# First norm tile by tile between modulation units, and the sum of squares inside the last unit

## The chip, the cores and the metric

The kernel runs on one core of one Trainium2 chip. The metric is the device time in microseconds of one execution; the time before is the median of three executions.

## The reference

Two blocks follow one another. The first is a two-layer transformer over a sequence of 256 tokens (x) and a context of 256 tokens (ctx), width 1024. The second is a two-layer attention network over x alone; the change does not touch it. What matters of the first block:

```
mod = silu(c) @ w_mod[i] + b_mod[i]          # 6 x 1024 per layer; mod_c the same from c_ctx
sh1, sc1, g1, sh2, sc2, g2 = split(mod, 6)
h  = rms_norm(x,  g_pre_mix) * (1 + sc1) + sh1        # "norm mix"
u  = h @ w_in                                          # kv, q, bc, xs0, ... in columns
y  = concat(attention, short conv, state space) @ w_out
x  = x + g1 * rms_norm(y, g_post_mix)                  # "post mix"
h  = rms_norm(x, g_pre_ffn) * (1 + sc2) + sh2          # "norm ffn"
x  = x + g2 * rms_norm(square(relu(h @ w_ff1)) @ w_ff2, g_post_ffn)   # "post ffn"
```

The context goes through the same steps with its own modulation in layer 0; in layer 1 only its mixer inputs are needed.

## The kernel before

Activations stand transposed: eight tiles k = 0 to 7 of 128 features by 512 tokens (context and x; 256 tokens where x alone is left, in layer 1). All large products are done in three matmuls, high part by high part, low by high, high by low (L976 to L978): every operand is split into a rounded half (hi) and the rest (lo). For weights ACT makes whi (L1498) and VectorE (DVE) makes wlo by a subtraction (L2048), half a unit at a time, into four buffers. For a normalised tile ACT makes HH (hi) and H32 (the full value), and DVE subtracts to HL (L2070).

The work is a list of steps, written out by hand, and each of the engines walks through the same list in order and does its own part of a step. A *unit* is 256 columns of a weight matrix: one load of 1 MB (SP's queue, three raw buffers, so a unit's load waits until the unit three places earlier has released its buffer), the splits, and matmuls over the eight k. A *modulation unit* (kind mod) is 256 columns of w_mod; its parts are steps of their own where the unit is alone: `mod_mm` (TensorE's matmuls from the raw weights, L1012), `mod_row` (ACT copies the row, L1683), `mod_pick` (TensorE turns the row into columns, L997), `mod_col` (DVE copies them, L2259). `fuse_pair j` (DVE, two small instructions) makes the scale and shift of tiles 2j and 2j+1 from units j and 4 + j.

In the first norm (layer 0, mix), units 0, 4, 1 and 5 have been made before, so tiles 0 to 3 can be modulated. `split_to` and `split_hi` split weight halves up to a number. A `norm` step lets DVE multiply tiles by the inverse root (XN, L2324) in groups (0), (1), (2, 3), (4, 5), (6, 7), ACT modulate them tile by tile (L1740, four activations a tile), and DVE subtract (HL) group by group. The step `one_k` does one k of the first two units, kv and q, 12 matmuls. The units 2, 6, 3 and 7, for tiles 4 to 7, are worked in between: matmuls after steps 0, 1 and 2, both picks of 2 and 6 after step 2, both of 3 and 7 after step 4. `norm` for tiles 4 and 5 stands ahead of step 4, that for 6 and 7 ahead of step 6. After these come the units bc, xs0, xs1 and so on. On SP's queue the loads stand in unit order: kv, q, 2, 6, 3, 7, bc, xs0, xs1; small constant tables go ahead of bc and ahead of xs1.

At the end of a sublayer (post mix after the four w_out units, post ffn after the last four w_ff2 units) the squares of the eight output tiles are summed. ACT squares a tile (L1523); DVE adds the squares of tiles 0 to 5 up in ACC; TensorE multiplies ACC, the square of tile 6 and the square of tile 7 by a matrix of ones into one bank (L1291, L1293, L1298); ACT takes the inverse root of it (RS, L1709) and DVE refines it (L2292 to L2294) and updates x (L2353, L2354). Before, ACC and the square of tile 6 are the step `post_part`, then come the matmuls of one modulation unit, then the square of tile 7 (`post`), then two more modulation units. After the last ffn there is no modulation unit. The norm that follows a post (`norm_sum`, `norm`) has the weight halves of the next two units split while the sum is made; DVE splits all of them ahead of the refinement.

Of the kernel before, what the change touches and what calls it, by code (L numbers as in the profile page):

```python
# [23 lines left out]
KC = D // P  # L24
# [5 lines left out]
LAYERS = 2  # L30
# [138 lines left out]
def build(nc, A, out, counts):  # L169
# [115 lines left out]
    s_sq = signal("sq")  # L285
# [74 lines left out]
    ones = place("ones_sb", [P, P])  # L360
# [101 lines left out]
    units, steps = [], []  # L462
# [89 lines left out]
    m = {}  # L552
# [12 lines left out]
    for i in (2, 6, 3, 7):  # L565
        m[i] = lone_mod(0, i)
    steps.append(("split_hi", 1))
    steps.append(("mod_mm", m[2]))
    steps.append(("norm", 0, "mix", (0, 1), 1))
    steps.append(("split_to", 3))  # L570
    steps.append(("norm", 0, "mix", (1, 4)))
    for k in range(KC):
        if k == 4:
            steps.append(("norm", 0, "mix", (4, 6)))
        if k == 6:
            steps.append(("norm", 0, "mix", (6, KC)))
        for u in (u_kv, u_q):
            steps.append(("one_k", u, k))
        if k in (0, 1, 2):
            steps.append(("mod_mm", m[(6, 3, 7)[k]]))  # L580
        if k in (1, 2):
            steps.append(("mod_row", m[(2, 6)[k - 1]]))
        if k == 2:
            for i in (2, 6):
                steps.append(("mod_pick", m[i]))
                steps.append(("mod_col", m[i]))
            steps.append(("fuse_pair", 2))
            steps.append(("mod_row", m[3]))
        if k == 4:
            steps.append(("mod_row", m[7]))  # L590
            for i in (3, 7):
                steps.append(("mod_pick", m[i]))
                steps.append(("mod_col", m[i]))
            steps.append(("fuse_pair", 3))
    for u in (u_kv, u_q):
# [16 lines left out]
    def gap_post(l, which, made):  # L612

        steps.append(("post_part", l, which))
        if made:
            steps.append(("mod_mm", made[0]))
        steps.append(("post", l, which))
        for u in made[1:3]:
            steps.append(("mod_mm", u))
        for u in made[:3]:  # L620
            steps.append(("mod_row", u))
            steps.append(("mod_pick", u))
# [187 lines left out]
    def t_of(l):  # L810
        return ALL if l == 0 else X
# [128 lines left out]
    def _(engine):  # L940
        pe = Waits(engine)
# [58 lines left out]
        def unit(u, halves=(0, 1), only=None):  # L1000
# [34 lines left out]
            for half in halves:  # L1035
# [7 lines left out]
                for bi, kk in turns:  # L1043
# [17 lines left out]
                    b = open_[(u.id, bi)]  # L1061
                    k = 4 * half + kk
                    pe.wait_ge(ready, ready.at(u.x[1:] + (k,)))
                    first, final = k == 0 and not (u.packed and bi == 1), k == KC - 1
# [221 lines left out]

        def post_part(l, which):
            t = t_of(l)
            b = acquire(7, (s_inv, ("p", l, which)))
            pe.wait_ge(s_acc, s_acc.at(("p", l, which, KC - 3)))  # L1290
            nc.tensor.matmul(b[:, 0:t[1] - t[0]], ones, ACC[:, t[0]:t[1]], start=True, stop=False)  # L1291
            pe.wait_ge(s_sq, s_sq.at(("p", l, which, KC - 2)))
            nc.tensor.matmul(b[:, 0:t[1] - t[0]], ones, SQ[0][:, t[0]:t[1]], start=False, stop=False)  # L1293

        def post(l, which):
            t = t_of(l)
            pe.wait_ge(s_sq, s_sq.at(("p", l, which, KC - 1)))
            nc.tensor.matmul(banks[7][:, 0:t[1] - t[0]], ones, SQ[1][:, t[0]:t[1]], start=False, stop=True)\  # L1298
                .then_inc(*s_norm_sum.tick(("p", l, which)))
# [111 lines left out]
        for st in steps:  # L1411
# [25 lines left out]
            elif kind == "consts":  # L1437
                engine.wait_ge(consts_in, 16 * CONSTS)
            elif kind == "post_part":
                post_part(*args)  # L1440
            elif kind == "post":
# [40 lines left out]
    def _(engine):  # L1482
# [243 lines left out]

        def norm(l, which, some, upto=-1):
            t = ALL if which == "mix" else t_of(l)
# [208 lines left out]
        for st in steps:  # L1937
# [24 lines left out]
            elif kind == "consts":  # L1962
# [4 lines left out]
                f(sel_r[0:48], sel[0:48], ACT.Copy).then_inc(*s_sel.tick(0))  # L1967
            elif kind == "norm":
                norm(*args)
# [65 lines left out]
    def _(engine):  # L2035
# [260 lines left out]
        def norm_sum(l, which, u1=None):  # L2296
            t = ALL if which == "mix" else t_of(l)
            sl = slice(t[0], t[1])
            if u1 is not None:
                splits(2 * u1.sid + 1)  # L2300
            refine(("n", l, which), banks[7][:, 0:t[1] - t[0]], RS[:, sl], ACC[:, sl], EPS)

        def norm(l, which, some, upto=-1):
            t = ALL if which == "mix" else t_of(l)
# [13 lines left out]

            groups = [g for g in ((0, 1), (1, 2), (2, 4), (4, 6), (6, 8)) if some[0] <= g[0] < some[1]]
            for n, (a_, b_) in enumerate(groups):  # L2320
# [5 lines left out]
                if t != ALL:  # L2326
# [5 lines left out]
                    ins.then_inc(*s_h32.tick(*((l, which, k) for k in range(a_, b_))))  # L2332
                splits(upto)
                if n >= 1:
# [296 lines left out]
        for at_step, st in enumerate(steps):  # L2631
# [25 lines left out]
            elif kind == "consts":  # L2657
                engine.wait_ge(consts_in, 16 * CONSTS)
                v.tensor_scalar(sinks8, sinks, 1.0 / SCALE, None, ALU.mult).then_inc(*s_sinks8.tick(0))
            elif kind == "norm":  # L2660
                norm(*args)
# [65 lines left out]
    def _(engine):  # L2727
# [15 lines left out]
        for st in steps:  # L2743
            kind, args = st[0], st[1:]
            pool.wait_ge(*so_far())
            if kind == "norm":
                l, which, some = args[:3]
# [80 lines left out]
```

## Time and profile before

| | |
|---|---|
| median of three runs | 1753.57 us (1753.41 to 1753.65) |
| profiled execution | 1752.07 us, span 1750.3 us |
| TensorE busy | 1578.8 us, 90% of the span |
| DVE, ACT busy | 985.2 us (56%), 916.1 us (52%) |
| mean granted TensorE clock | 0.938 |
| share of the last chain | PE 70%, ACT 13%, DVE 12% |

The span runs from the first to the last instruction of the profiled execution. Busy times of engines overlap. The granted clock is a share of 2.4 GHz, of which 0.50 is 1.2 GHz. A matmul's listed duration contains its run-out, so the starts tell how fast they follow one another. The full-precision matmul of a sum is listed as two passes.

### The profile page before, as it was taken

The numbers are of one execution on the slowest core, as the hardware profiler recorded it, in microseconds if no ns is written. First come the engines' busy times: TensorE is split into PE (matmuls) and PEld (weight loads), VectorE is DVE, ScalarE is ACT, GpSimd is POOL, SyncE is SP. The second block draws the span as 40 slices with busy tenths as digits, with TensorE's granted clock in tenths as the row PEclk, the third lists the DMA queues.
The fourth block names the chain that finished last, engine by engine and source line by source line (L and its number), as shares of the span: only waits on it lengthen the run. The fifth ranks groups of instructions, "written<-read, shape, count | busy, mean of one in ns | idle before, by whom it ended". The sixth has DMA issues, their size and how long they took to land.

```text
span 1750.3 us, 25703 instructions
## 1 busy us (share of the span) xinstructions
PE 1578.8 (90%) x10227; PEld 1323.4 (76%) x10227; DVE 985.2 (56%) x1596; ACT 916.1 (52%) x1516; POOL 62.3 (4%) x82
## 2 busy tenths in 40 slices
PE   5799898879999999979978889998999998887697
PEld 3588455647888888847855789998989898786587
DVE  2264565555343434464755576667675666576655
ACT  5453554446232323455555455556776766376646
POOL 3000033000000000000003000000000000000000
PEclk9899987899999999989996899999999999998899
DMA  7532434341323232342305456663634443242232
GB/s 241 163 103 89 140 119 151 125 150 63 121 97 97 96 98 95 113 135 73 121 25 193 153 170 195 195 198 127 222 127 139 145 142 124 97 154 88 73 121 73
DMA packets 223641, 225.40 MB, mean 129 GB/s; under 512 B 8235, under 2 KB 222065, under 8 KB 223473
## 3 DMA queue, kind: packets, MB, share of 16 engines
q1 hardware_dynamic: 222816, 223.63, 39.9%
q8 instruction: 81, 1.33, 0.3%
q14 instruction: 40, 0.32, 0.1%
q0 software_dynamic: 704, 0.12, 0.0%
HBM read 222.68 MB, written 1.05 MB: 128 GB/s over the span
## 4 chain that ended last, share of the span: by engine, by line
PE 70%; ACT 13%; DVE 12%; issue 2%; POOL 1%; DMA 1%; DVEq 0%; ACTq 0%; POOLq 0%
PE bank L976 19%; PE bank L978 19%; PE bank L977 19%; ACT whi L1498 2%; DVE wlo L2048 2%; PE bank L1284 2%; PE bank L1012 1%; ACT SH L1634 1%; ACT H L1740 1%; ACT HH L1740 1%; PE bank L997 1%; ACT AP L1904 1%; PE bank L1262 1%; PE bank L1177 1%; DVE AP L2573 1%
## 5 line engine op out<-in xcount | busy, mean ns | idle before, releaser
L2048 DVE TENSOR_TENSOR wlo<-raw,whi 128x1024 fp32r<-128x1024 f32 (+2 forms) x322 | 388.8, 1208 | 319.0 <-ACT whi L1498 314.7
L1498 ACT ACTIVATE whi<-raw 128x1024 fp32r<-128x1024 f32 (+2 forms) x322 | 336.9, 1047 | 303.8 <-PE bank L978 285.9
L976 PE MATMUL bank<-HH,whi 128*128 128x512 f32 (+2 forms) x640 | 247.6, 387 | 32.0 <-DVE HL L2070 30.3
L977 PE MATMUL bank<-HL,whi 128*128 128x512 f32 (+2 forms) x640 | 244.1, 381 | 0.0
L978 PE MATMUL bank<-HH,wlo 128*128 128x512 f32 (+2 forms) x640 | 243.8, 381 | 0.0
L976 PE MATMUL bank<-HA,whi 128*128 128x256 f32 x576 | 165.4, 287 | 18.9 <-DVE wlo L2048 8.9
L976 PEld LDWEIGHTS bank<-HH,whi 128*128 128x128 f32 (+1 forms) x640 | 122.4, 191 | 62.0 <-issue 20.6
L977 PE MATMUL bank<-LA,whi 128*128 128x256 f32 x576 | 162.3, 282 | 0.0
L978 PE MATMUL bank<-HA,wlo 128*128 128x256 f32 x576 | 162.1, 281 | 0.0
L978 PEld LDWEIGHTS bank<-HH,wlo 128*128 128x128 f32 (+1 forms) x640 | 122.2, 191 | 24.2 <-issue 1.1
L977 PEld LDWEIGHTS bank<-HL,whi 128*128 128x128 f32 (+1 forms) x640 | 122.5, 191 | 23.5 <-issue 1.4
L976 PEld LDWEIGHTS bank<-HA,whi 128*128 128x128 f32 x576 | 111.3, 193 | 22.9 <-issue 12.0
L977 PEld LDWEIGHTS bank<-LA,whi 128*128 128x128 f32 x576 | 111.6, 194 | 0.0
L978 PEld LDWEIGHTS bank<-HA,wlo 128*128 128x128 f32 x576 | 111.3, 193 | 0.0
L976 PE MATMUL bank<-FH,whi 128*128 128x512 f32 x256 | 99.7, 390 | 0.0
L977 PE MATMUL bank<-FL,whi 128*128 128x512 f32 x256 | 99.6, 389 | 0.0
L978 PE MATMUL bank<-FH,wlo 128*128 128x512 f32 x256 | 99.6, 389 | 0.0
L976 PE MATMUL bank<-HX,whi 128*128 128x256 f32 x320 | 91.7, 287 | 4.1 <-DVE HXL L2070 4.1
L977 PE MATMUL bank<-HXL,whi 128*128 128x256 f32 x320 | 90.9, 284 | 0.0
L978 PE MATMUL bank<-HX,wlo 128*128 128x256 f32 x320 | 90.8, 284 | 0.0
L976 PE MATMUL bank<-YH,whi 128*128 128x256 f32 x264 | 79.3, 300 | 7.8 <-DVE YL L2721 4.5
L1634 ACT ACTIVATE SH<-bank 32x512 f32<-32x512 f32 (+1 forms) x116 | 67.5, 582 | 18.7 <-PE bank L978 17.3
(371 smaller groups left out, 3220.1 us busy)
## 6 DMA issues: line engine op xcount, KB each, us to landing
raw<-in_w_ff_dram SPq DMA_DIRECT2D x64, 1024.0 KB, 5.3
raw<-in_w_mod_dram SPq DMA_DIRECT2D x48, 1024.0 KB, 5.2
raw<-in_a_w_in_dram SPq DMA_DIRECT2D x40, 1024.0 KB, 5.0
raw<-in_w_in_dram SPq DMA_DIRECT2D x18, 1024.0 KB, 5.4
raw<-in_b_w_in_dram SPq DMA_DIRECT2D x9, 1024.0 KB, 5.3
raw<-in_w_out_dram SPq DMA_DIRECT2D x8, 1024.0 KB, 5.1
raw<-in_ple_w_gate_dram SPq DMA_DIRECT2D x8, 1024.0 KB, 5.4
raw<-in_a_w_out_dram SPq DMA_DIRECT2D x4, 1024.0 KB, 5.1
```

The source lines that it names most:

```text
L976: nc.tensor.matmul(o, wh, xh, start=start, stop=False, skip_group_check=shared)
L977: nc.tensor.matmul(o, wh, xl, start=False, stop=False, skip_group_check=shared)
L978: return nc.tensor.matmul(o, wl, xh, start=False, stop=stop, skip_group_check=shared)
L997: ins = nc.tensor.matmul(b[:, 2 * j:2 * j + 2], mrow[mod_no[key] % 3][:, j * P:(j + 1) * P], pick, start=True, stop=True)
L1012: ins = nc.tensor.matmul(b[32 * q:32 * q + 32, 0:256], cs[:, k, :], raw[u.id % RAW_SLOTS][:, k * 256:k * 256 + 256], start=turn == 0, stop ...
L1177: ins = nc.tensor.matmul(b[:, 0:SEQ], VV[:, kt, (h // 2) * P:(h // 2) * P + P], PT[(i - 3) % 2][:, kt, :], start=kt == 0, stop=kt == nt - 1)
L1262: ins = nc.tensor.matmul(b[64 * e:64 * e + 64, c * P - t0:c * P - t0 + P], w[:, c, f:f + 64], of[(2 * p + e) % 4][:, ts_], start=w is XTK, ...
L1284: nc.tensor.matmul(b[:, 0:t[1] - t[0]], ones, SQ[k % 2][:, t[0]:t[1]], start=k == 0, stop=k == KC - 1)\
L1498: f(whi[h % HALF_SLOTS][:, 0:n], raw[u.id % RAW_SLOTS][:, (h % 2) * n:(h % 2) * n + n], ACT.Copy)\
L1634: ins = f(SH[sh_turn[0] % 2][32 * q:32 * q + 32, 0:n, :], b[32 * o:32 * o + 32, 0:n, :], ACT.Copy)
L1740: ins = f(dst, XN[n][:, k % 2, ts_], ACT.Identity, scale=fA[:, k, 1 - s:2 - s], bias=modT[l][:, a + k, 1 - s:2 - s])
L2048: v.tensor_tensor(wlo[h % HALF_SLOTS][:, 0:n], raw[u.id % RAW_SLOTS][:, (h % 2) * n:(h % 2) * n + n], whi[h % HALF_SLOTS][:, 0:n].bitcast( ...
```

## The change

Three edits.

In the first norm the step `norm` is parted into `norm_dve` and `norm_act`, and the order is written anew: DVE multiplies tile by tile, with weight halves split between tiles up to the numbers given; ACT modulates tiles 0, 1 to 2, 3, 4 to 5 and 6 to 7 in steps of their own; the four modulation units follow one another between the steps of kv and q, each one's row and pick between tiles, and `fuse_pair` follows at once.

At the later norms the sum of ACC moves into the sublayer's last unit (`post_acc`, ahead of the last quarter of its matmuls); squares 6 and 7 form `post`, and all three modulation units come after them.

In layer 1's ffn norm DVE splits only the first half of the second unit's weights ahead of the refinement; the second half falls to the next unit's step.

```diff
-    steps.append(("split_hi", 1))
-    steps.append(("mod_mm", m[2]))
-    steps.append(("norm", 0, "mix", (0, 1), 1))
-    steps.append(("split_to", 3))
-    steps.append(("norm", 0, "mix", (1, 4)))
-    for k in range(KC):
-        if k == 4:
-            steps.append(("norm", 0, "mix", (4, 6)))
-        if k == 6:
-            steps.append(("norm", 0, "mix", (6, KC)))
+    def one_k(k):
+
         for u in (u_kv, u_q):
             steps.append(("one_k", u, k))
-        if k in (0, 1, 2):
-            steps.append(("mod_mm", m[(6, 3, 7)[k]]))
-        if k in (1, 2):
-            steps.append(("mod_row", m[(2, 6)[k - 1]]))
-        if k == 2:
-            for i in (2, 6):
-                steps.append(("mod_pick", m[i]))
-                steps.append(("mod_col", m[i]))
-            steps.append(("fuse_pair", 2))
-            steps.append(("mod_row", m[3]))
-        if k == 4:
-            steps.append(("mod_row", m[7]))
-            for i in (3, 7):
-                steps.append(("mod_pick", m[i]))
-                steps.append(("mod_col", m[i]))
-            steps.append(("fuse_pair", 3))
+
+    def mod_parts(i, *kinds):
+
+        for kind in kinds:
+            steps.append((kind, m[i]))
+
+    steps.append(("split_hi", 1))
+    mod_parts(2, "mod_mm")
+    steps.append(("norm_dve", 0, "mix", (0, 4), (1, 1, 3, 3)))
+    steps.append(("norm_act", 0, "mix", (0, 1)))
+    mod_parts(2, "mod_row", "mod_pick")
+    steps.append(("split_hi", 3))
+    steps.append(("norm_act", 0, "mix", (1, 3)))
+    one_k(0)
+    mod_parts(6, "mod_mm", "mod_row")
+    steps.append(("norm_act", 0, "mix", (3, 4)))
+    one_k(1)
+    mod_parts(2, "mod_col")
+    mod_parts(6, "mod_pick", "mod_col")
+    steps.append(("fuse_pair", 2))
+    steps.append(("norm_dve", 0, "mix", (4, 6), (3, 3)))
+    steps.append(("norm_act", 0, "mix", (4, 6)))
+    one_k(2)
+    mod_parts(3, "mod_mm", "mod_row")
+    one_k(3)
+    mod_parts(3, "mod_pick", "mod_col")
+    mod_parts(7, "mod_mm", "mod_row")
+    one_k(4)
+    mod_parts(7, "mod_pick", "mod_col")
+    steps.append(("fuse_pair", 3))
+    steps.append(("norm_dve", 0, "mix", (6, KC), (3, 3)))
+    steps.append(("norm_act", 0, "mix", (6, KC)))
+    for k in range(5, KC):
+        one_k(k)
...
     def gap_post(l, which, made):
 
-        steps.append(("post_part", l, which))
-        if made:
-            steps.append(("mod_mm", made[0]))
         steps.append(("post", l, which))
-        for u in made[1:3]:
+        for u in made[:3]:
             steps.append(("mod_mm", u))
...
                     k = 4 * half + kk
+                    if k == 4 and bi == 1 and (u.kind, u.key) in post_at:
+                        post_acc(*post_at[u.kind, u.key])
...
-        def post_part(l, which):
+        post_at = {("wout", (l, 3)): (l, "mix") for l in range(LAYERS)}
+        post_at.update({("ff2", (l, 3, 3)): (l, "ffn") for l in range(LAYERS)})
+
+        def post_acc(l, which):
+
             t = t_of(l)
             b = acquire(7, (s_inv, ("p", l, which)))
             pe.wait_ge(s_acc, s_acc.at(("p", l, which, KC - 3)))
             nc.tensor.matmul(b[:, 0:t[1] - t[0]], ones, ACC[:, t[0]:t[1]], start=True, stop=False)
-            pe.wait_ge(s_sq, s_sq.at(("p", l, which, KC - 2)))
-            nc.tensor.matmul(b[:, 0:t[1] - t[0]], ones, SQ[0][:, t[0]:t[1]], start=False, stop=False)
 
         def post(l, which):
             t = t_of(l)
+            pe.wait_ge(s_sq, s_sq.at(("p", l, which, KC - 2)))
+            nc.tensor.matmul(banks[7][:, 0:t[1] - t[0]], ones, SQ[0][:, t[0]:t[1]], start=False, stop=False)
...
             if u1 is not None:
-                splits(2 * u1.sid + 1)
+                splits(2 * u1.sid + (0 if (l, which) == (1, "ffn") else 1))
...
-            groups = [g for g in ((0, 1), (1, 2), (2, 4), (4, 6), (6, 8)) if some[0] <= g[0] < some[1]]
+            groups = [(0, 1), (1, 2), (2, 4), (4, 6), (6, 8)] if ups is None else [(k, k + 1) for k in range(*some)]
...
-                splits(upto)
+                if ups is not None:
+                    splits(ups[n])
```

## Rows read from the trace of the kernel before

**Rows 1.** Waits of PE, 30 to 84: in total, times, longest.

```profile
PE bank L976 <- DVE HL L2070: 12.9, 5, 4.6
```

**Rows 2.** Windows: length; PE, PEld, DVE, ACT, POOL busy (count); clock; DMA share; GB/s.

```profile
39.00:43.00 4.00, 4.00 (x10) 2.73 (x11) 3.71 (x4) 1.67 (x4) 0.00 (x0) 0.50 0.80 253
43.00:57.50 14.50, 13.60 (x96) 8.44 (x94) 4.27 (x8) 7.20 (x17) 0.00 (x0) 1.00 1.07 354
57.50:62.20 4.70, 0.19 (x1) 0.00 (x0) 1.23 (x1) 3.82 (x9) 0.00 (x0) 0.78 0.93 213
62.20:66.70 4.50, 4.45 (x11) 3.08 (x12) 0.00 (x0) 0.00 (x0) 0.00 (x0) 0.50 0.10 12
```

**Rows 3.** Timeline of PE, first norm: start, duration, instruction [idle before it and its releaser].

```profile
38.93 0.77 PE L976 MATMUL bank<-HH,whi 128*128 128x512 f32 x1 [2.86 <-DVE HL L2070]
...
43.76 1.07 PE L1012 MATMUL bank<-raw,silu_c_wide 128*32 128x256 f32 x16
...
49.77 0.50 PE L976 MATMUL bank<-HH,whi 128*128 128x512 f32 x1 [0.44 <-DVE HL L2070]
...
52.42 0.40 PE L978 MATMUL bank<-HH,wlo 128*128 128x512 f32 x1
...
53.75 1.05 PE L997 MATMUL bank<-pick,mod_row 128*128 128x2 f32 x8
...
83.57 0.39 PE L976 MATMUL bank<-HH,whi 128*128 128x512 f32 x1
```

**Rows 4.** Timeline of ACT, first norm.

```profile
38.09 2.01 ACT L1498 ACTIVATE whi<-raw 128x1024 fp32r<-128x1024 f32 x2
...
44.42 1.08 ACT L1740 ACTIVATE HH<-XN,modT,fuse_scale 128x256 fp32r<-128x256 f32 x2
...
60.97 0.38 ACT L1683 ACTIVATE mod_row<-bank 128x256 f32<-128x256 f32 x1
```

**Rows 5.** Timeline of DVE, first norm.

```profile
38.09 0.69 DVE L2070 TENSOR_TENSOR HL<-H,HH 128x512 fp32r<-128x512 f32 x1 [0.63 <-ACT H L1740]
39.25 2.36 DVE L2048 TENSOR_TENSOR wlo<-raw,whi 128x1024 fp32r<-128x1024 f32 x2 [0.47 <-ACT whi L1498]
...
54.91 0.16 DVE L2259 COPY modT<-bank 128x4 f32<-128x4 f32 x1 [0.29 <-PE bank L997]
```

**Rows 6.** Timeline of SP's queue: the issue that begins with the load of xs1.

```profile
62.17 27.55 SPq L870 DMA_DIRECT2D raw<-in_w_in_dram  x3
```

**Rows 7.** DMA issues, 61 to 63 us: size, us to landing (the load of xs1).

```profile
raw<-in_w_in_dram SPq DMA_DIRECT2D x1, 1024.0 KB, 13.0
```

**Rows 8.** Timeline around the post of layer 0, mix.

```profile
367.16 1.02 PE L1291 MATMUL bank<-ACC,ones_sb 128*128 128x512 f32 x2
...
368.02 1.02 PE L1293 MATMUL bank<-SQ,ones_sb 128*128 128x512 f32 x2
...
368.13 0.63 ACT L1523 ACTIVATE SQ<-YM 128x512 f32<-128x512 f32 x1 [2.02 <-DVE YM L2132]
...
369.97 1.12 PE L1298 MATMUL bank<-SQ,ones_sb 128*128 128x512 f32 x2
```

**Rows 9.** Timelines around the three later posts: layer 0 ffn, layer 1 mix, layer 1 ffn.

```profile
750.95 0.63 ACT L1523 ACTIVATE SQ<-YM 128x512 f32<-128x512 f32 x1 [2.02 <-DVE YM L2171]
...
753.24 1.13 PE L1298 MATMUL bank<-SQ,ones_sb 128*128 128x512 f32 x2
...
995.23 0.86 ACT L1523 ACTIVATE SQ<-YM 128x256 f32<-128x256 f32 x2 [3.38 <-DVE YM L2128]
...
997.33 0.70 PE L1298 MATMUL bank<-SQ,ones_sb 128*128 128x256 f32 x2
...
1191.37 0.59 PE L1291 MATMUL bank<-ACC,ones_sb 128*128 128x256 f32 x2
```

**Rows 10.** Timeline of ACT and DVE at the norm of layer 1, ffn.

```profile
1008.71 0.47 ACT L1709 ACTIVATE RS<-bank,eps_c 128x256 f32<-128x256 f32 x1
...
1009.92 0.42 DVE L2292 SCALAR_TENSOR_TENSOR ACC<-RS 128x256 f32<-128x256 f32 x1
```

More of the change, by code:

```diff
@@ L1438, in _ @@
                 engine.wait_ge(consts_in, 16 * CONSTS)
-            elif kind == "post_part":
-                post_part(*args)
             elif kind == "post":
@@ L1725, in norm_sum, with norm @@
                 half_root(s_norm_sum, ("n", l, which), banks[7][:, 0:t[1] - t[0]], RS[:, sl], 0)
-        def norm(l, which, some, upto=-1):
+        def norm(l, which, some):
             t = ALL if which == "mix" else t_of(l)
@@ L1967, in _ @@
                 f(sel_r[0:48], sel[0:48], ACT.Copy).then_inc(*s_sel.tick(0))
-            elif kind == "norm":
+            elif kind in ("norm", "norm_act"):
                 norm(*args)
@@ L2299, in norm_sum, with norm @@
             if u1 is not None:
-                splits(2 * u1.sid + 1)
+                splits(2 * u1.sid + (0 if (l, which) == (1, "ffn") else 1))
             refine(("n", l, which), banks[7][:, 0:t[1] - t[0]], RS[:, sl], ACC[:, sl], EPS)
-        def norm(l, which, some, upto=-1):
+        def norm(l, which, some, ups=None):
             t = ALL if which == "mix" else t_of(l)
@@ L2659, in _ @@
                 v.tensor_scalar(sinks8, sinks, 1.0 / SCALE, None, ALU.mult).then_inc(*s_sinks8.tick(0))
-            elif kind == "norm":
+            elif kind in ("norm", "norm_dve"):
                 norm(*args)
@@ L2745, in _ @@
             pool.wait_ge(*so_far())
-            if kind == "norm":
+            if kind in ("norm", "norm_dve"):
                 l, which, some = args[:3]
```

## The prediction, made before the changed kernel was run

> **What bounds the kernel now.** I read the slices of the page first: TensorE is the busy engine nearly everywhere, and the dips of its granted clock are the places to look at. The change touches three: the first norm (slices 1 and 2), the four joints where a sublayer's output is normalised, and the norm ahead of layer 1's first ff1 unit. Next come the waits of TensorE between 30 and 84 us [rows 1]: it waited 12.9 us, five times, for HL, the low half of a normalised tile. One of the five is the first tile at 38.93, 2.86 us [rows 3], which stays; 10.0 us are left, nearly all in two waits of up to 4.6 us. The windows show what such a wait costs beyond itself [rows 2]: from 57.5 to 62.2 the engine is busy 0.19 us, and from 62.2 to 66.7 it works at 0.50, which is 1.2 GHz, so 4.5 us do the work of 2.25. The second wait (tiles 6 and 7) is followed by such a stretch too. From 39 to 43 the clock is low as well, and that stays. So some 10.0 + 2 x 2.25 = 14.5 us can be won in this stage, and its other rows show the order that costs it: ACT turns a tile in 2.0 us (two pairs, 1.08 each, slightly overlapped) [rows 4], but may start a pair of tiles only after the picks of two modulation units, which stand behind a whole step, and TensorE then waits for both tiles and one joint subtraction.
>
> **The first norm, step by step.** Nothing is removed: the same four units (matmuls, row copies, picks, column copies), the same 32 activations of ACT, the same 96 matmuls of the two units kv and q. What is added is small: single tiles where pairs were taken together, 0.69 us for a subtraction [rows 5], and I take the multiplication (XN), of the same shape, as the same.
> Start: ACT ends tile 0 at 38.09, then copies unit 2's row, 0.38, and TensorE picks it, half of 1.05 [rows 3, 4]; step 0 starts at about 39.0 instead of 38.93. I cost that at 0.1.
> Steps 0 to 3: ACT then splits two weight halves (2.01), and ends tile 1 at 42.5 and tile 2 at 44.5 [rows 4]; with the wlo pair (2.36) and the HL of 0.69 on DVE [rows 5] tile 1 is there at 43.2 and tile 2 at 45.2. Step 0 ends near 44 as before, since the matmuls of unit 6 followed it at 43.76 with no wait for their load [rows 3], and that load is asked for at the same time as now. ACT copies unit 6's row only when these matmuls end (about 45.1), so tile 3 is ready at 45.5 + 2.0 + 0.7 = 48.2. TensorE asks for tiles 1, 2 and 3 at about 45, 48.4 and 52.4 (a step is 2.65 to its last matmul's start, with that matmul 2.9 [rows 3]; a unit's matmuls 1.0): no wait.
> Tiles 4 and 5: unit 6's pick ends at 48.4; then a column copy of 0.16 [rows 5], two more such small instructions, XN 0.69, ACT 2.0, HL 0.69, with some 0.3 of hand-overs 4.1 in all. Tile 4 is ready at 52.5, tile 5 two later; they are wanted at 57 and 60: no wait. The row of unit 3 stands behind them on ACT, about 54.2; its pick comes after step 3, at 55.1.
> Tiles 6 and 7: unit 7's pick can end at 60.0 at the earliest, and the same 4.1 follows; beside it lies only step 5, 2.9. I expect one wait of 1.2 to 1.3 ahead of step 6, none ahead of step 7. The clock should stay at 2.4 GHz from 43 on: in the window from 43 to 57.5 it read 1.00 [rows 2] although step 2 began after a break of 0.44 [rows 3].
> So the stage gives 14.5 - 0.1 - 1.3 = 13.1 us. Added up from the front, step 7 ends near 70.2 instead of 83.57 [rows 3], 13.4; I take 13.2. The bounds: 14.5 if the last wait vanishes too, and 11 if it takes the clock down with it.
> On SP the loads keep their order, but that of xs0 now waits for unit 3's matmuls, three us later than before, and with it the small tables and xs1 behind them. xs1 was asked for at 62.17 and took 13.0 [rows 6, 7]; it would land near 78. TensorE wants it two units (of four steps' matmuls, 11 us each) after 70.2, at 92. The cover is over 10 us: cost nothing. Gone, it would cost ACT its place in the queue first, and TensorE us for us after that.
>
> A rule speaks against the shorter pieces. The row first: with the unit matmuls between the steps the granted clock was 1.00 from 43 to 57.5 [rows 2]. The Trainium skill, "TensorE: Matmul & The Clock Gate", section "A second HAM failure mode: psum-queue depth-cycling", tells of a kernel whose many short idle times between groups of matmuls made the clock swing between its two rates. By that rule the stage would run at 1.2 GHz and the time come out as in the slowest of the rivals below, by the row as in the sum; the trace agrees with the row's side here, at 1.00.
>
> **The joints.** The matmul of the accumulated squares (ACC) moves into the last unit, ahead of its last quarter, and the first modulation unit's matmuls move behind the last square's matmul. TensorE works in order, so the last block of the unit ends later by ACC: 0.86 for 512 columns (367.16 to 368.02) [rows 8], about half of that for 256, and so does the copy and the square of tile 7. ACC itself must be ready there: its last addition depends only on the unit before. In return the last square's matmul no longer waits behind 1.0 us of modulation.
> Layer 0, mix: square 7 ended at 368.76, now 369.62; its matmul started at 369.97 [rows 8]. Gain 0.3. Layer 0, ffn: 751.58 + 0.86 = 752.44 against 753.24 [rows 9]: 0.8. Layer 1, mix: the pair of squares ended at 996.09, plus 0.43 is 996.5, and square 6's matmul ends at about 996.7, against 997.33 [rows 9]: 0.55. Layer 1, ffn has no modulation unit: there ACC, 0.43 (row of 0.59 with its tail), stood in idle time and now doesn't: -0.4 [rows 9]. Together 1.25. Bounds: a loss of 2 x 0.86 + 2 x 0.43 = 2.6 if nothing comes back, a gain of 3 if all three units' 1.0 does.
> **The later split.** In layer 1's ffn norm RS was ready at 1009.18, but DVE began its refinement at 1009.92 [rows 10], held by the split of a weight half that now comes after the norm. Gain 0.7; TensorE wants that half only 24 short matmuls into the second unit, so DVE has time. Bounds 0 and 0.7.
>
> **Sum.** 13.2 + 1.25 + 0.7 = 15.2. The profiled execution took 1752.07 (span 1750.3 and 1.8 around it), 1.5 under the median of the three runs shown, 1753.57. So 1736.9 by its own time, 1738.3 as a median. After the stage TensorE is the bound and later loads are released by its own progress, so I expect no part to be given back.
>
> **Rivals.**
> *The clock falls at the one wait left* (1.3 us ahead of step 6). Between the break of 0.44 that kept the clock and the wait of 4.6 that lost it the rows decide nothing. Price 2.2 [rows 2]: 1740.5.
> *A load comes late.* xs1, or one of units 6, 3 and 7, takes longer than its cover, and ACT, working in order, holds a tile behind a row. For: 13.0 us for a load of 1 MB [rows 7]. Against: 43.76 without a wait [rows 3]. With some 4 us lost: 1742.
> *The move into the last unit does not do what it says*: it hides nothing, since the block after it ends later, and the gain from the modulation unit is not on the path. Then -2.6 instead of +1.25: 1742.2.
> *Slower: the stage at 1.2 GHz throughout.* 96 matmuls at 0.43 (11 took 4.45 us at that clock [rows 2]; twice a warm step's 0.24 is the most) are 41 us, the three units and picks after step 0 about 6: from 39 to 86.4, 2.9 later than 83.57; less the 1.9 of the other parts, 1754.5. It is slower than before by more than the bound below if the low clock holds over five more us of the next unit, 1757. For: breaks at every step. Against: 1.00 in the window that has such breaks [rows 2].
>
> **How the numbers follow.** Forecast 0.74, its own range 1736 to 1740.5; the clock at the last wait 0.12; a late load 0.04; the joints 0.06; the slow stage 0.04. About 0.2%, 3.5 us, is what a measurement of this kernel can tell from no change. The first four are all faster by more than that: 0.96; the slow stage is half within, half over: 0.02 and 0.02. The low end is the sum of the upper bounds, 14.5 + 3 + 0.7 = 18.2, 1735.4, with a little for the runs: 1734. The high end takes in the late load and the joints, and both a lost clock and a dead joint: 1744.
>
> **What would show it.** TensorE's waits for HL between 30 and 72 fall to about 4.2, the first included; the granted clock reads 1.00 from 43 to the end of the stage, or 0.50 after a wait near 63 if the first rival holds; the copy of the kv unit's result starts about 13 us earlier; the last square's matmul starts 0.3, 0.8 and 0.55 earlier, and 0.4 later, counted from the start of the sublayer's last unit. The forecast is wrong if a wait of several us for a row, a pick or a load stands between the steps.

## The result, and the profile after

The changed kernel took 1735.88 us (median of four, 1733.42 to 1739.19), the kernel before beside it 1753.49 (1751.25 to 1753.65): a ratio of 0.9904, interval 0.989 to 0.9918. The forecast was 1738.3, its range 1734 to 1744. With all the runs of the two kernels that the experiments brought, the kernel before spreads over 10.6 us and the changed one over 6.7, so what a part is worth has to be read from its place in the trace, and only the whole from the times. Two executions of kernels below took 3871 and 5280 us, where the others of the same two kernels took 1734 to 1749, and are left out of every number.

| | before | after |
|---|---|---|
| profiled execution, span | 1752.07, 1750.3 | 1735.26, 1733.5 |
| TensorE busy | 1578.8 (90%) | 1572.1 (91%) |
| mean granted clock | 0.938 | 0.945 |
| first norm: from its inverse root (ACT, RS) to the copy of the kv unit's result (ACT, CK) | 49.56 | 35.78 |

After, the waits of TensorE from 30 to 75 us, which answer to [rows 1] (the first two stand ahead of the stage's first tile):

```profile
PE bank L1019 <- DMA raw<-in_w_mod_dram: 3.0, 1, 3.0
PE bank L1004 <- ACT mod_row L1694: 2.1, 1, 2.1
PE bank L983 <- DVE HL L2081: 1.5, 1, 1.5
```

Five waits for HL have become one; the first tile's wait, 2.86 before, is now one of 2.1 for the row ahead of the pick. The windows of [rows 2], same columns, after:

```profile
39.00:43.00 4.00, 4.00 (x12) 2.84 (x13) 3.09 (x4) 3.97 (x8) 0.00 (x0) 0.57 0.72 246
43.00:57.50 14.50, 14.50 (x102) 9.46 (x101) 5.70 (x13) 8.76 (x18) 0.00 (x0) 1.00 1.06 351
57.50:62.20 4.70, 4.70 (x24) 3.62 (x22) 1.78 (x5) 1.03 (x3) 0.00 (x0) 1.00 0.97 227
62.20:66.70 4.50, 2.96 (x14) 2.00 (x13) 1.68 (x3) 4.08 (x8) 0.00 (x0) 1.00 0.10 12
```

From 43 on the clock (last but two) reads 1.00, and the third window, in which TensorE had 0.19 us to do, is full. The fourth holds the one wait that is left; it did not take the clock down. PE's timeline after, the rows that answer to [rows 3]:

```profile
38.41 1.01 PE L1004 MATMUL bank<-pick,mod_row 128*128 128x2 f32 x4 [2.15 <-ACT mod_row L1694]
39.28 0.77 PE L983 MATMUL bank<-HH,whi 128*128 128x512 f32 x1
...
43.69 1.07 PE L1019 MATMUL bank<-raw,silu_c_wide 128*32 128x256 f32 x16
...
64.03 0.50 PE L983 MATMUL bank<-HH,whi 128*128 128x512 f32 x1 [1.54 <-DVE HL L2081]
```

And DVE's, to [rows 5]: single tiles' HL, the column copies of units 2 and 6 together, that of unit 7.

```profile
42.53 0.69 DVE L2081 TENSOR_TENSOR HL<-H,HH 128x512 fp32r<-128x512 f32 x1 [0.69 <-ACT H L1751]
...
48.16 0.36 DVE L2270 COPY modT<-bank 128x4 f32<-128x4 f32 x2
...
51.93 0.69 DVE L2081 TENSOR_TENSOR HL<-H,HH 128x512 fp32r<-128x512 f32 x1 [1.69 <-ACT H L1751]
...
59.71 0.16 DVE L2270 COPY modT<-bank 128x4 f32<-128x4 f32 x1 [4.17 <-PE bank L1004]
...
63.28 0.69 DVE L2081 TENSOR_TENSOR HL<-H,HH 128x512 fp32r<-128x512 f32 x1 [1.68 <-ACT H L1751]
```

Each tile came within 0.2 us of the forecast: tile 1 there at 43.2, tile 4 at 52.6 (52.5 forecast), tile 6 at 64.0 (64.1). ACT's timeline shows the stage's two ends and xs1, whose load it waited for until 75.63 (forecast near 78) while TensorE went on (it has no wait from 70 to 100 us); asked for at 62.21, it took 13.3, close to the 13.0 of [rows 6, 7]:

```profile
32.08 0.69 ACT L1720 ACTIVATE RS<-bank,eps_c 128x512 f32<-128x512 f32 x1
...
67.86 0.60 ACT L1574 ACTIVATE CK<-bank 128x512 f32<-128x512 f32 x1 [1.55 <-PE bank L985]
...
75.63 1.06 ACT L1509 ACTIVATE whi<-raw 128x1024 fp32r<-128x1024 f32 x1 [1.55 <-DMA raw<-in_w_in_dram]
```

The joints on PE, answering to [rows 8, 9]: square 7's matmul (L1311), now waiting for its square and for nothing else in layer 0, and the modulation behind it. (The bare times can't be set beside those of before, since all of it begins earlier; the next section takes distances.)

```profile
355.53 1.13 PE L1311 MATMUL bank<-SQ,ones_sb 128*128 128x512 f32 x2 [0.63 <-ACT SQ L1534]
356.58 2.80 PE L1019 MATMUL bank<-raw,silu_c_wide 128*32 128x256 f32 x48
...
737.98 1.12 PE L1311 MATMUL bank<-SQ,ones_sb 128*128 128x512 f32 x2 [0.19 <-ACT SQ L1534]
```

And the later split, to [rows 10]: 0.50 from the inverse root (ACT) at 985.82 to this first instruction of the refinement (DVE), where it was 1.21.

```profile
986.32 0.42 DVE L2303 SCALAR_TENSOR_TENSOR ACC<-RS 128x256 f32<-128x256 f32 x1
```

### The profile page after: what moved, and what is told of

The parts are those of the page before. It is cut to its first block, busy times and chain, and to the rows that moved or that the text cites. A ratio compares the mean times of both kernels' runs of the same rounds, so it can differ in the third digit from the quotient of the medians.

```text
span 1733.5 us, 25713 instructions
## 1 busy us (share of the span) xinstructions
PE 1572.1 (91%) x10227; PEld 1324.0 (76%) x10227; DVE 986.4 (57%) x1602; ACT 916.2 (53%) x1516; POOL 63.3 (4%) x82
## 4 chain that ended last, share of the span: by engine, by line
PE 73%; ACT 12%; DVE 11%; issue 2%; POOL 1%; DMA 1%; DVEq 0%; ACTq 0%; POOLq 0%
PE bank L983 20%; PE bank L985 20%; PE bank L984 20%; ACT whi L1509 2%; DVE wlo L2059 1%; PE bank L1019 1%; PE bank L1293 1%; ACT AP L1915 1%; ACT SH L1645 1%; ACT H L1751 1%; PE bank L1004 1%; ACT HH L1751 1%; PE bank L1363 1%; PE bank L1186 1%; DVE AP L2585 1%
## 5 line engine op out<-in xcount | busy, mean ns | idle before, releaser
L983 PE MATMUL bank<-HA,whi 128*128 128x256 f32 x576 | 169.1, 294 | 18.5 <-DVE wlo L2059 8.7
L984 PE MATMUL bank<-LA,whi 128*128 128x256 f32 x576 | 166.1, 288 | 0.0
L985 PE MATMUL bank<-HA,wlo 128*128 128x256 f32 x576 | 165.8, 288 | 0.0
L983 PEld LDWEIGHTS bank<-HH,whi 128*128 128x128 f32 (+1 forms) x640 | 121.4, 190 | 49.5 <-issue 18.3
L983 PEld LDWEIGHTS bank<-HA,whi 128*128 128x128 f32 x576 | 114.8, 199 | 22.2 <-issue 11.9
L985 PEld LDWEIGHTS bank<-HA,wlo 128*128 128x128 f32 x576 | 114.9, 200 | 0.0
```

Of the source, the lines that this page charges most:

```text
L983: nc.tensor.matmul(o, wh, xh, start=start, stop=False, skip_group_check=shared)
L984: nc.tensor.matmul(o, wh, xl, start=False, stop=False, skip_group_check=shared)
L985: return nc.tensor.matmul(o, wl, xh, start=False, stop=stop, skip_group_check=shared)
```

## The experiments

The theory after the first comparison: the first norm gave 13.8, the joints 1.4, the later split 0.7, and what is over is the clock, which dips elsewhere in each execution. The rivals: the modulation behind the last square also keeps the clock up at the next norm; and of each edit only one half does the work.

**The same kernel again.** No edit.

> The changed kernel once more, nothing edited. Theory (first norm 13.8 us, joints 1.4, later split 0.7, and the rest of the first comparison is wander of the clock in stretches that the change doesn't touch): about 1736 us; in its profile the first norm and the joints stand as in the first profile within 0.2 us, while the stretches where the two first profiles differed most, the state-space part of layer 1 (836 to 958 in the kernel before, 3.2 us faster there) and the second block's attention (6.4 us slower), take other lengths, each off by 2 us or more in one of them. Rival (the modulation matmuls that now stand nearer to the sum of the next norm keep TensorE's clock up there, always): the sum of squares after layer 0's ffn is again about 7.3 us long and that after layer 1's mix about 3.6.

Measured: 1735.43 (six, 1733.04 to 1739.77), the kernel before on this chip 1751.77 (23 runs, 1747.32 to 1756.99), ratio 0.9905 [0.9889, 0.9922]. First norm 36.76 instead of 35.78, with the same waits of 3.0 and 1.5; its window from 43 to 57.5 read 0.94, since the clock came back later after step 0. Two windows of the first profile, from the inverse root of layer 1's first norm to that of its post mix, and all behind the last inverse root:

```profile
755.13:976.49 221.36, 188.60 (x1168) 145.73 (x1171) 131.63 (x242) 124.09 (x229) 18.47 (x22) 0.91 0.35 110
1172.14:1733.50 561.36, 495.11 (x4004) 469.20 (x4004) 359.06 (x642) 356.65 (x590) 0.00 (x0) 0.93 0.38 123
```

and the same two of the second:

```profile
757.41:982.73 225.32, 194.96 (x1168) 149.12 (x1172) 131.22 (x242) 124.41 (x228) 17.67 (x22) 0.87 0.34 108
1178.10:1738.00 559.90, 490.36 (x4004) 464.32 (x4004) 359.19 (x642) 356.76 (x590) 0.00 (x0) 0.94 0.38 123
```

One program, the same instructions, 4.0 us longer in one stretch and 1.5 shorter in the other, with the clock (0.91 and 0.87, 0.93 and 0.94) going along. In the kernel before:

```profile
771.56:998.07 226.51, 197.33 (x1184) 151.52 (x1187) 130.81 (x242) 124.33 (x229) 17.54 (x22) 0.88 0.34 107
1194.13:1750.30 556.17, 486.90 (x4004) 460.31 (x4004) 359.12 (x642) 356.50 (x590) 0.00 (x0) 0.94 0.38 124
```

So of the 5.2 us that the first comparison had gained in the first stretch the repeat kept 1.2, about what the joint at its end is worth (1.3 beside this profile, as the table below shows). The second stretch was 5.2 longer than before in the first profile and still 3.7 longer in the repeat. Its code is the same in all kernels; it took 556.1 to 558.6 in the four profiles with at most one of the edits, and in the eight that have the first two, whole or in part, 557.2 once and 559.9 to 562.1 otherwise. That no edit lengthens it is not shown, and what would is open. The posts came out alike to 0.01 us, and the sum after layer 0's ffn at 7.34 beside 7.31: that part of the rival stood.

**One edit at a time.** The diffs are the three parts of the change, each on the kernel before.

> The first edit alone (first norm tile by tile with the units between) on the kernel before. Theory: 13.8 us off the kernel before, 1739.7, all of it ahead of the copy of the kv unit's result (81.76 before, near 67.9 now); the joints and the later split as before. Rival (the joints' new order is worth 3 to 4 us by the clock): then this one is 3 to 4 us slower than the changed kernel beside the 0.7 of the split, so 1740 to 1741 and over.

> The second edit alone (sum of ACC inside the last unit, modulation matmuls behind the last square) on the kernel before. Theory: 0.3 + 0.75 + 0.75 - 0.4 = 1.4 us off, 1752.1. Rival (the clock stays up at the next norm's sum): 3 to 4 us off, 1749.5 to 1750.5, with the sum of squares after layer 0's ffn near 7.3 us instead of 8.5. Rival (the move hides nothing): 2.6 us slower, 1756.

> The third edit alone (second half of the second unit's weights split after layer 1's ffn norm) on the kernel before. Theory: 0.7 us between RS and DVE's refinement (1.21 before, 0.50 then), all of it reaching TensorE's first matmul of the unit: 1752.8, which no time can tell from the kernel before, but the trace can. Rival (the split comes late for the second unit and TensorE waits for it instead): the 0.7 comes back as a wait for wlo within the next 25 us.

Measured, all beside the 1751.77: first norm alone 1737.38, ratio 0.9919 [0.9898, 0.9941]; joints alone 1748.55, 0.9974 [0.996, 0.9988]; split alone 1752.48, 1.0005 [0.9993, 1.0017]. The joints alone brought more than the 1.4 of the theory. The places say why. I measure from DVE's copy of the sublayer's first square into ACC to the inverse root of the post, and from there to that of the next norm:

| kernel | layer 0 mix, norm after | layer 0 ffn, norm after | layer 1 mix, norm after | layer 1 ffn |
|---|---|---|---|---|
| before | 33.93, 16.04 | 34.38, 17.16 | 18.16, 10.64 | 16.40 |
| first norm alone | 33.93, 16.03 | 34.38, 17.14 | 17.51, 10.28 | 16.39 |
| split alone | 33.93, 16.04 | 34.39, 17.13 | 17.52, 9.33 | 16.40 |
| joints alone | 33.69, 15.91 | 33.69, 16.03 | 16.82, 9.32 | 16.81 |
| after | 33.68, 15.90 | 33.69, 15.98 | 16.82, 9.33 | 16.82 |
| ACC out (below) | 32.78, 15.95 | 33.19, 14.97 | 16.33, 9.33 | 16.38 |
| unit between (below) | 33.98, 16.01 | 34.44, 17.07 | 18.59, 9.33 | 16.81 |

The distances up to three of the posts repeat to 0.02 us, so small terms can be read that no time shows. The one up to layer 1's mix does not: before, with one unit between and with pairs (17.37, a kernel below), TensorE's matmuls of the w_out units started 0.118 us apart, in the nine other profiles 0.113 apart (medians), although the clock read 1.00 in all twelve. Why is open. So the old joint there is the 17.51 of the two other kernels and not the 18.16. The posts gained 0.25, 0.69, 0.69 and lost 0.42, 1.2 in all. But the norm after layer 0's ffn is 1.1 shorter as well, wherever the new joints are. In the trace of the joints alone, PE:

```profile
754.23 2.80 PE L1009 MATMUL bank<-raw,silu_c_wide 128*32 128x256 f32 x48
757.09 1.50 PE L994 MATMUL bank<-pick,mod_row 128*128 128x2 f32 x12
760.66 7.34 PE L1283 MATMUL bank<-SQ,ones_sb 128*128 128x512 f32 x12 [2.08 <-ACT SQ L1722]
```

and before:

```profile
754.30 1.93 PE L1012 MATMUL bank<-raw,silu_c_wide 128*32 128x256 f32 x32
757.15 1.50 PE L997 MATMUL bank<-pick,mod_row 128*128 128x2 f32 x12 [0.92 <-ACT mod_row L1683]
760.73 8.47 PE L1284 MATMUL bank<-SQ,ones_sb 128*128 128x512 f32 x12 [2.08 <-ACT SQ L1721]
```

The sum starts at the same distance behind the same wait of 2.08, but its 12 passes take 8.47 instead of 7.34. Windows from the post's inverse root on, before:

```profile
754.40:760.00 5.60, 3.33 (x44) 2.25 (x44) 4.67 (x6) 3.47 (x9) 0.00 (x0) 0.99 1.00 317
760.00:764.00 4.00, 3.27 (x4) 1.46 (x5) 3.93 (x4) 1.74 (x3) 0.00 (x0) 0.50 1.05 333
764.00:767.40 3.40, 3.40 (x6) 1.34 (x5) 3.30 (x6) 1.27 (x3) 0.00 (x0) 0.61 0.03 11
```

and with the joints alone:

```profile
754.34:759.94 5.60, 4.19 (x60) 2.76 (x59) 4.67 (x6) 3.48 (x9) 0.00 (x0) 1.00 0.63 198
759.94:763.94 4.00, 3.28 (x4) 1.36 (x5) 3.93 (x4) 1.73 (x3) 0.00 (x0) 0.60 1.10 349
763.94:767.34 3.40, 3.40 (x8) 1.12 (x7) 3.30 (x6) 2.40 (x4) 0.00 (x0) 0.96 0.61 192
```

With 16 matmuls more behind the last square TensorE is busy 4.19 instead of 3.33 us ahead of the sum, the clock falls later and is back sooner (0.96 where 0.61 stood).

The split alone started the refinement 0.7 us sooner, but the time doesn't show it; more of it below. The sum after layer 1's mix, which the first rival also named, took 3.64 in this kernel too, which has the old joints, so they can come out as short. But the two other kernels with the old joints took 4.90 and 4.65, and all nine profiles with the second edit, whole or in part, 3.63 or 3.64: whether the edit has a part in it stays open.

**Which half of the first edit: tiles or places.**

```diff
-            groups = [...] if ups is None else [(k, k + 1) for k in range(*some)]
+            groups = [...] if ups is None else [some] if some[0] >= 4 else [(k, k + 1) for k in range(*some)]
```

> The changed kernel, but tiles 4 and 5, and 6 and 7, are again taken as pairs by DVE (multiplication and subtraction); the places of the units, rows and picks stay. Theory (single tiles are what makes the last wait short): no wait for tiles 4 and 5 (ready near 56, wanted at 57), but the pair 6 and 7 is ready only about 7.7 us after unit 7's pick, so TensorE waits about 4.3 us ahead of step 6 and none ahead of step 7, and 2.9 us are lost against the changed kernel's 1.54 and more; if the clock falls after that wait as it did in the kernel before, 2.2 more. So the copy of the kv unit's result 2.9 to 5.1 us later than the changed kernel's. Rival (the places alone do it): no more than 0.5 us later.

And single tiles in the old order of steps:

```diff
+    steps.append(("norm", 0, "mix", (1, 4), (3, 3, 3)))
+    for k in range(KC):
+        if k == 4:
+            steps.append(("norm", 0, "mix", (4, 6), (3, 3)))
+        if k == 6:
+            steps.append(("norm", 0, "mix", (6, KC), (3, 3)))
...
```

> The changed kernel, but in the first norm the units, rows and picks stand in the places of the kernel before (picks of two units together after steps 2 and 4, norm steps not parted), while DVE works tile by tile. Theory (what costs in the kernel before is the pair, not the place): two waits for HL of about 1.3 us, ahead of steps 4 and 6, where the changed kernel has one, and the clock at 1.00; the copy of the kv unit's result 1 to 1.5 us later than the changed kernel's, so most of the 13.8 us is kept. Rival (the place of the picks is what matters): waits of 3 us and more ahead of steps 4 and 6 and a fall of the clock after them, 6 us or more later.

Measured beside 1753.12 for the kernel before: pairs 1742.56 (five), ratio 0.9937 [0.9916, 0.9958]; old places 1738.78, 0.991 [0.9893, 0.9928]. The stage's distance was 41.39 with pairs and 38.59 in the old places, where the kernels with the whole edit have 35.78 to 36.76. PE's wait with pairs, and windows around it:

```profile
68.36 0.72 PE L983 MATMUL bank<-HH,whi 128*128 128x512 f32 x1 [4.57 <-DVE HL L2081]
```

```profile
62.20:66.70 4.50, 1.58 (x7) 0.95 (x6) 0.64 (x1) 3.69 (x8) 0.00 (x0) 1.00 0.15 14
...
68.30:71.50 3.20, 3.14 (x8) 2.07 (x9) 1.23 (x2) 0.00 (x0) 0.00 (x0) 0.53 0.36 111
```

One wait of 4.57 and 1.2 GHz behind it, as before: 5.2 us over the mean of the whole edit, 36.2 over five profiles (35.78, 36.76, 36.22, 36.07, 35.96), at the upper end of what was expected. In the old places:

```profile
45.19 0.50 PE L973 MATMUL bank<-HH,whi 128*128 128x512 f32 x1 [0.54 <-DVE HL L2071]
58.60 0.50 PE L973 MATMUL bank<-HH,whi 128*128 128x512 f32 x1 [1.52 <-DVE HL L2071]
66.86 0.50 PE L973 MATMUL bank<-HH,whi 128*128 128x512 f32 x1 [1.54 <-DVE HL L2071]
```

Windows of the same kernel around the last two:

```profile
57.50:62.20 4.70, 3.60 (x20) 2.87 (x20) 1.49 (x3) 2.68 (x6) 0.00 (x0) 1.00 0.88 207
...
66.70:70.90 4.20, 4.04 (x18) 2.91 (x19) 2.02 (x3) 2.62 (x5) 0.00 (x0) 1.00 0.34 103
```

The clock read 1.00 in spite of both waits of 1.5. The stage lost 2.4 us, more than the 1 to 1.5 expected: the 0.54 for tile 1 had not been counted, and the two waits were 1.5 and not 1.3. So each half alone brings most of the 13 us (8 for the places, 11 for the tiles); both halves shorten the same waits, and they don't add. (With pairs, tiles 2 and 3 were still taken one by one, so the 8 may hold a little of the other half.)

**Which half of the second edit.** ACC back behind the unit:

```diff
-                    if k == 4 and bi == 1 and (u.kind, u.key) in post_at:
-                        post_acc(*post_at[u.kind, u.key])
...
         def post(l, which):
             t = t_of(l)
+            post_acc(l, which)
```

> The changed kernel, but the sum of ACC stands again behind the last unit, ahead of squares 6 and 7, and all three modulation units stay behind the last square. Theory (of the second edit the modulation behind the square gains, and ACC inside the unit costs what it delays): inverse roots, counted from the last unit's start, earlier than in the changed kernel by 0.7 (layer 0 mix), 0.3 (layer 0 ffn), 0.3 (layer 1 mix) and 0.4 (layer 1 ffn), 1.7 in all, and the sum of squares after layer 0's ffn stays at 7.3 us. Rival (ACC inside is what gains): inverse roots later, by up to 0.9 each.

Or one unit's matmuls back between the squares (post_part being square 6 alone, and the ACC still inside):

```diff
+        steps.append(("post_part", l, which))
+        if made:
+            steps.append(("mod_mm", made[0]))
         steps.append(("post", l, which))
-        for u in made[:3]:
+        for u in made[1:3]:
```

> The changed kernel, but one modulation unit's matmuls stand again between squares 6 and 7, with ACC still inside the last unit. If the modulation behind the last square is what keeps the clock up at the next sum, the 12 passes of that sum after layer 0's ffn take 8.5 us again instead of 7.3, and the inverse roots of layer 0 and of layer 1's mix come as late as in the kernel before, 0.3, 0.7 and 0.75 later than now: 3 us slower than the changed kernel in these places. If ACC inside is what keeps it up, the sum stays at 7.3.

Measured beside the same 1753.12: 1738.59 (five), ratio 0.991 [0.9891, 0.9928], and 1740.81, 0.9926 [0.9908, 0.9944]; neither time parts them from the changed kernel, the table does. ACC out: every post is earlier, by 0.90, 0.50, 0.49 and 0.44, 2.3 in all, against the 1.7 expected. PE at layer 0's mix:

```profile
353.79 1.02 PE L1302 MATMUL bank<-ACC,ones_sb 128*128 128x512 f32 x2
354.65 1.02 PE L1308 MATMUL bank<-SQ,ones_sb 128*128 128x512 f32 x2
355.50 1.06 PE L1310 MATMUL bank<-SQ,ones_sb 128*128 128x512 f32 x2
```

The three follow one another with no wait here: ACC fills the time in which tile 7 is copied and squared. With one unit between, all that the joints had won is gone, and the sum after layer 0's ffn takes 8.39 again:

```profile
743.49 1.50 PE L1007 MATMUL bank<-pick,mod_row 128*128 128x2 f32 x12 [0.92 <-ACT mod_row L1702]
747.07 8.39 PE L1296 MATMUL bank<-SQ,ones_sb 128*128 128x512 f32 x12 [2.08 <-ACT SQ L1740]
```

So of the second edit the modulation behind the last square gains, at both ends, and ACC inside the unit costs 2.3.

**A version that follows from it.** ACC out, and units 3 and 7 one step earlier:

```diff
+    mod_parts(3, "mod_mm", "mod_row")
     steps.append(("norm_dve", 0, "mix", (4, 6), (3, 3)))
     steps.append(("norm_act", 0, "mix", (4, 6)))
     one_k(2)
-    mod_parts(3, "mod_mm", "mod_row")
-    one_k(3)
     mod_parts(3, "mod_pick", "mod_col")
     mod_parts(7, "mod_mm", "mod_row")
-    one_k(4)
+    one_k(3)
     mod_parts(7, "mod_pick", "mod_col")
...
-    for k in range(5, KC):
+    for k in range(4, KC):
```

> Two edits on the changed kernel: ACC's sum stands behind the last unit (as in the run before this), and in the first norm units 3 and 7 are worked one step earlier (unit 3 ahead of step 2, unit 7 behind it, unit 7's pick after step 3). Theory: unit 7's pick then ends about 4 us earlier, tiles 6 and 7 are there when wanted, the last wait of 1.54 us goes and the copy of the kv unit's result comes 1.5 us earlier (34.3 to 35.2 us after the first inverse root, where the changed kernel had 35.8 and 36.8); the joints again 3.3 better than the changed kernel's (inverse roots 0.90, 0.50, 0.49 and 0.44 earlier, the sum after layer 0's ffn 1.05). Together 4.8 under the changed kernel, about 1731. Rival (load of unit 3 or 7 comes too late for the earlier place): a wait of TensorE for one of them and no gain in the first norm.

And the same without the third edit:

```diff
-                splits(2 * u1.sid + (0 if (l, which) == (1, "ffn") else 1))
+                splits(2 * u1.sid + 1)
```

> The same, with the third edit undone: in layer 1's ffn norm DVE again splits both halves of the second unit ahead of the refinement. Theory (the 0.7 us that the later split gains ahead of the first tile is lost again, since the tiles that follow are worked at 1.2 GHz for longer): from the norm's inverse root to the copy of the first ff1 unit 13.5 us, where the kernels with the later split have 13.7 to 14.3; nothing to be seen in the time, or up to 0.8 us less. Rival (the 0.7 is kept): 0.7 longer than in the run before this one.

Measured: 1733.8, ratio 0.9889 [0.9869, 0.9908], and 1735.13, 0.9894 [0.9876, 0.9913], both beside 1754.24 for the kernel before. The intervals overlap that of the changed kernel: the times don't tell the version from it, and that it is faster rests on the places. TensorE waits for no tile after the first; what is left behind step 0 is 0.3 for a bank:

```profile
PE bank L1018 <- DMA raw<-in_w_mod_dram: 3.0, 1, 3.0
PE bank L1003 <- ACT mod_row L1692: 1.6, 1, 1.6
PE bank L1018 <- DVE modT L2268: 0.3, 1, 0.3
```

But the stage took 35.54, not 34.3 to 35.2, for the clock came back later, near 45.2 and so ahead of the first edited step (0.92 from 43 to 57.5; the profile without the third edit has the same 0.92, and 35.52). The posts stood at 32.78, 33.18, 16.33 and 16.38, 2.3 better than in the changed kernel as before; the norm after layer 0's ffn at 15.90, so the 14.97 with ACC out was the clock's and not the edit's. The norm after layer 0's mix took 16.03 in both, as before, so the 0.1 by which it was shorter in the table may not be the edit's.

The split: from the norm's inverse root to the copy of the first ff1 unit's result I expected 13.5 without it and found 15.31, against 14.23 with it. That is the rival's side, here: the refinement had begun 1.64 and 0.51 behind the inverse root, and nearly all of that came through. But over all profiles the eight with the split have 12.84 (the kernel with pairs, which my expectation had left out) to 14.30, mean 13.9, and the four without 13.46, 13.81, 13.97 and 15.31, mean 14.1: my reason, that the split itself lengthens the slow stretch, falls, and a gain of 0.7 can't be told from this spread either. TensorE waits for the first tile there, then works at 1.2 GHz for 3 to 10 us, and when that ends moves by more than 0.7 from one execution to the next. What the split is worth stays open.

## Why the prediction was right

**The first norm** carried it, by the mechanism forecast. Forecast -13.2 (with 0.1 of it lost at the start); measured 49.56 to 35.78 in the first pair, and 49.5 (49.56, 49.97, 48.94 in the three profiles with the old stage) to 36.2 over all: -13.3. The wait that was left was 1.54 instead of 1.2 to 1.3, step 0 began at 39.28 and not at 39.0, and the clock was back a little sooner, which made up for it. The clock at the low level was priced from [rows 2] as half the work of a stretch, and that held: of the 10.0 us of waits 8.5 went, and the rest of the 13.3, 4.8, is near the 4.5 priced for the two stretches behind them. TensorE's waits for HL fell to 1.5 and not to 4.2 with the first included, since the first tile is now there before the pick ahead of it ends.

**The rival of the clock at the last wait** could not be decided from the rows of before, between breaks of 0.44 and 4.6. It didn't come: 1.00 after 1.54 here, after 1.52 and 1.54 in the old places, 0.53 after 4.57 with pairs. **The slower rival** (the stage at 1.2 GHz throughout) had the Trainium skill's page "TensorE: Matmul & The Clock Gate", section "A second HAM failure mode: psum-queue depth-cycling", beside it. The Trainium skill tells there of a swing; the prediction priced its extreme. The stage with units and picks between its steps came back to 1.00 between 42 and 46 us in every profile that has it, and stayed there unless a wait of 4.57 came (pairs): no run here shows that swing in it.

**A late load** did not come either: xs1 was there at 75.6, and TensorE had work to 80 and over.

**The joints** were forecast as 0.3, 0.8, 0.55 and -0.4 and came as 0.25, 0.69, 0.69 and -0.42, 1.2 against 1.25 (the third counted from 17.51). The step that was missing is what the moved modulation does behind the post: some 1.1 us less at the norm after layer 0's ffn, by the clock (17.1 to 17.2 in the four profiles without it, 15.0 to 16.0 in the eight with it), and perhaps 0.1 at the norm after its mix. The second edit is so worth some 2.4 and not 1.25; its own time, 0.9974, lies on that side. And the prediction took the two halves of the edit as one trade, while the runs show one that gains some 4.7 (2.4 + 2.3) and one that costs 2.3.

**The later split** is the term that the runs don't bear out: the refinement starts 0.7 sooner, as forecast, but the end of the unit lies anywhere in a spread of 2.5 us, and neither a gain of 0.7 nor none is shown.

Summed by what the runs showed, 13.3 + 2.4 and nothing certain for the split are 15.7, beside 15.2 forecast and 17.6 measured in the first four runs, 16.3 in the second comparison. That the forecast sum came so near is in part luck: the joints were 1.2 too low by the missing step, and the split's 0.7 is not seen. The rest of the difference is within the wander of kernels whose single executions lie 7 us and more apart. "No part to be given back" is not settled: the total shows no loss, but the second block was 557.4 us long on average in the four profiles with at most one edit and 560.7 in the eight others, with its code unchanged.

## What to carry to other kernels

A wait is worth more than its length when the clock falls behind it, and cutting a batch of tiles into single tiles, or placing its producers earlier, both do that: try the cheaper one first, they don't add. Work that doesn't depend on the critical sum belongs behind it, and in this kernel a partial sum that is ready early belongs into the idle time ahead of its last term, and not into the dense work before, where it delays everything. Where executions wander by more than the effect, measure the distance between two events of the same stage in several profiles; in dense stages it repeats to hundredths where the total doesn't repeat to microseconds. One profile is not enough: one of the four distances here had two levels, 0.6 us apart.

## What the runs showed of the hardware

The span of one program wandered by 4.5 us between two profiles (1733.5 and 1738.0), although a stretch of 366.6 us with a dense TensorE, from the inverse root of layer 0's ffn norm to that of its post, repeated to 0.02 us. The wander lay in the stretches where TensorE waits often, for the most part with the granted clock going along. So a rise or fall of the clock at a given place need not follow from any edit: the sum after layer 1's mix took 4.90 before and 3.64 with the split alone, whose edit lies behind it.

A clock that reads 1.00 is not yet one speed: in layer 1's w_out units the matmuls started 0.113 us apart in nine profiles and 0.118 in three, both at 1.00. No run here shows why.

Also unexpected: the fourth modulation unit's load of the norm came late, a wait that the kernel before did not have. All eight profiles with the three units behind the last square have it (0.58 to 1.62), the split alone a short one (0.22); the first norm alone and the kernel with one unit between don't.

```profile
986.39 1.07 PE L1019 MATMUL bank<-raw,silu_c_wide 128*32 128x256 f32 x16 [0.61 <-DMA raw<-in_w_mod_dram]
989.83 0.36 PE L983 MATMUL bank<-HX,whi 128*128 128x256 f32 x1 [2.38 <-DVE HXL L2081]
```

It cost nothing, since TensorE had to wait 2.38 more for the first tile behind it.
